# Last norm, router and ranks as one flow, a ring of eight expert weights, and expert rows stored from ScalarE's queue

## What is computed

```
h2 = rms_norm(xl, norm2_gain) * (1.0 + sc2) + sh2          # 512 tokens x 1024
g_logits = h2 @ w_rg + b_rg                                 # 4 groups
e_logits = h2 @ w_re + b_re                                 # 4 groups x 8 experts
g_sel = argmax(g_logits); g_w = softmax(g_logits)[g_sel]
top_w, top_i = top_k(softmax(e_logits[g_sel]), 2)           # two experts of the chosen group
top_w = top_w / sum(top_w) * g_w
y = sum over the two experts e: top_w[e] * ((silu(h2 @ w_gate[e]) * (h2 @ w_up[e])) @ w_down[e])
xl = xl + g2 * y
```

## Time and profile before

| | us |
|---|---|
| median of 3 runs | 2468.18 (2465.8 to 2471.98) |
| profiled execution, its own time | 2464.07 |
| its span, first to last instruction | 2462.2 |
| TensorE matmul busy | 2201.4 (89% of the span) |
| VectorE busy | 900.0 (37%) |
| ScalarE busy | 509.3 (21%) |
| GpSimd busy | 121.4 (5%) |

### The profile page before, as it was taken

One profiled execution on the slowest core, in us unless ns is written; L12 is line 12 of the kernel. 1 busy time (PEld: TensorE's weight loads), 2 busy tenths in 40 slices (PEclk: granted clock), 3 DMA queues, 4 the chain that ended last, 5 costly groups with the idle time before them and its releaser, 6 DMA issues. The chain is left out here.

```text
span 2462.2 us, 35642 instructions
## 1 busy us (share of the span) xinstructions
PE 2201.4 (89%) x15256; PEld 1344.8 (55%) x15256; DVE 900.0 (37%) x1867; ACT 509.3 (21%) x1036; POOL 121.4 (5%) x152
## 2 busy tenths in 40 slices
PE   7999999888998998999999787896976699999995
PEld 3445575445775343585865454783874454444442
DVE  3661064324333013068335556537544411111102
ACT  1000161131122012242112545224211010000001
POOL 0000000004210000000000000300400000000001
PEclk9999999999999999999999998888976799999997
DMA  3222201100003851111130000000004599999995
GB/s 131 77 77 77 77 2 43 61 30 27 28 28 111 343 187 43 43 52 35 44 125 26 1 1 27 3 14 14 4 18 179 210 405 427 426 427 426 428 426 234
DMA packets 48205, 328.45 MB, mean 133 GB/s; under 512 B 5552, under 2 KB 10288, under 8 KB 33840
## 3 DMA queue, kind: packets, MB, share of 16 engines
q1 hardware_dynamic: 46896, 321.96, 33.5%
q0 software_dynamic: 1152, 4.19, 0.5%
HBM read 311.45 MB, written 14.68 MB: 132 GB/s over the span
## 5 line engine op out<-in xcount | busy, mean ns | idle before, releaser
L3188 PE MATMUL psum<-m_ring,m_xg 128*64 128x512 f32 x1024 | 230.3, 604 | 19.9 <-issue 18.7
L258 PE MATMUL psum<-h,wring 128*128 128x512 f32 (+1 forms) x448 | 172.8, 535 | 16.8 <-PEq L93 12.4
L481 PE MATMUL psum<-h,wring 128*128 128x512 f32 x384 | 167.7, 600 | 7.2 <-PEq L93 7.2
L3188 PEld LDWEIGHTS psum<-m_ring,m_xg 128*64 128x64 f32 x1024 | 79.5, 139 | 167.6 <-issue 166.3
L3173 PE MATMUL psum<-m_sel,m_htok 128*128 128x128 f32 x1024 | 122.8, 279 | 17.8 <-DVE m_sel L3164 17.8
L3173 PEld LDWEIGHTS psum<-m_sel,m_htok 128*128 128x128 f32 x1024 | 118.5, 194 | 30.4 <-DVE m_sel L3164 18.2
L258 PEld LDWEIGHTS psum<-h,wring 128*128 128x128 f32 x448 | 84.3, 194 | 84.0 <-issue 73.5
L481 PEld LDWEIGHTS psum<-h,wring 128*128 128x128 f32 x384 | 73.9, 193 | 101.0 <-issue 101.0
L3214 PE MATMUL psum<-m_ring,m_hid_t 128*64 128x512 f32 x512 | 115.0, 602 | 0.9 <-ACT m_hid_t L3312 0.9
L3198 DVE TENSOR_TENSOR m_hid<-m_sg,psum 64x512 f32<-64x512 f32 x32 | 22.1, 691 | 227.4 <-ACT m_sg L3194 227.4
L2293 PE MATMUL psum<-h,wring 128*128 128x256 f32 (+1 forms) x288 | 96.5, 486 | 1.3 <-PEq L93 1.2
(11 more groups left out here) (566 smaller groups left out, 3597.9 us busy)
## 6 DMA issues: line engine op xcount, KB each, us to landing
m_ring<-in_w_gate SPq DMA_DIRECT2D x32, 2048.0 KB, 23.4
m_ring<-in_w_up SPq DMA_DIRECT2D x32, 2048.0 KB, 22.4
m_ring<-in_w_down SPq DMA_DIRECT2D x32, 2048.0 KB, 20.4
wring<-in_w1f SPq DMA_DIRECT2D x60, 512.0 KB, 3.6
ada_ring<-in_w_ada SPq DMA_DIRECT2D x12, 2048.0 KB, 10.3
wring<-in_w2f SPq DMA_DIRECT2D x31, 512.0 KB, 3.5
expert_rows<-m_rows SPq DMA_DIRECT2D x16, 512.0 KB, 22.9
wring<-in_w1v SPq DMA_DIRECT2D x12, 512.0 KB, 3.5
```

The source lines that it names most:

```text
L258: m = nc.tensor.matmul(place(t, out), lhs, rhs, start=(k == 0), stop=(k == KD - 1))
L481: m = nc.tensor.matmul(K.psum[:, banks[t % 4]], ws.weights(first + t, k), h[:, k], start=(k == 0), stop=(k == KD - 1))
L3188: m = nc.tensor.matmul(K.psum[i * SLOTS:(i + 1) * SLOTS, UP + s], W.xg[:, k, s], w[:, k], start=(k == 0), stop=(k == KD - 1))
```

## The change

`last_norm` takes in the logits and the transposes. Tile by tile: VectorE scales into one of four slots, ScalarE adds the shift, TensorE multiplies the tile as moving operand by the router's matrix (one matmul of 36 rows x 512 columns) and turns its four blocks, and VectorE copies the turned tile while it scales the next. The logits come out with experts on partitions; ScalarE adds the bias, four small transposes turn them back, and VectorE copies them (`lg`). The router follows in the same stage and no second stage is opened. It picks the group's logits with two instructions in place of seven and hands over the sum of both choices. The ranks come from four matmuls (up to 128 columns), the totals from four more. `rank` is now one higher, and the slots that it is compared with too (`count1`).

The rest of `place` (positions, further lots) becomes a generator whose five pieces VectorE runs in the experts' stage, one in each of the first five pairs, between its selection and the copy of the rows. Clearing the spare rows moves to the stage `po2`. The ring has eight slots. The row store is issued by ScalarE, after it has copied the next pair's gathered tokens. The buffers `sg` and `rows` now lie in `rstd` and `tmp`, and `hm` has four tiles in place of eight, which frees the space for the slot.

```diff
-def last_norm(nc, K, x, out, gain, shift, bank, loads, weights):
+def last_norm(nc, K, x, hm, h_tok, gain, shift, wr, br, lg_t, lg, count1, loads, weights):
+    SUMS, LOGITS, BACK, NB = 7, 0, 1, 4
+    slot = lambda k: hm[:, k % NB]
+    bank = lambda k: 2 + k % NB
...
     def scalar(eng, sem):
         yield 0.0
-        roots(nc, eng, sem, K, bank, S, 0, 0)
+        roots(nc, eng, sem, K, SUMS, S, 0, 0)
         for k in range(KD):
             eng.wait_ge(sem["scaled"], k + 1)
-            nc.scalar.activation(out(k), out(k), ACT.Identity, bias=shift[:, k:k + 1])
+            nc.scalar.activation(slot(k), slot(k), ACT.Identity, bias=shift[:, k:k + 1]).then_inc(sem["normed"], 1)
+        eng.wait_ge(sem["loaded"], 16 * len(loads))
+        eng.wait_ge(sem["summed"], 1)
+        nc.scalar.activation(lg_t, K.psum[:n_lg, LOGITS], ACT.Identity, bias=br).then_inc(sem["biased"], 1)
+
+    def tensor(eng, sem):
+        yield 0.0
+        eng.wait_ge(sem["loaded"], 16 * len(loads))
+        for k in range(KD):
+            eng.wait_ge(sem["normed"], k + 1)
+            m = nc.tensor.matmul(K.psum[:n_lg, LOGITS], wr[:, k], slot(k), start=(k == 0), stop=(k == KD - 1))
...
+            for t in range(TT):
+                m = nc.tensor.transpose(K.psum[:, bank(k), t * P:(t + 1) * P], slot(k)[:, t * P:(t + 1) * P], K.ident)
+            m.then_inc(sem["turned"], 1)
+        eng.wait_ge(sem["biased"], 1)
+        for t in range(TT):
+            m = nc.tensor.transpose(K.psum[:, BACK, t * n_lg:(t + 1) * n_lg], lg_t[:, t * P:(t + 1) * P], K.ident[:n_lg, :n_lg])
+        m.then_inc(sem["back"], 1)
...
-    return Program(["loaded", "rooted", "scaled"], sync=sync, scalar=scalar, vector=vector)
+        for k in range(NB):
+            scale(k)
+        for k in range(KD - 1):
+            copy(k)
+            if k + NB < KD:
+                scale(k + NB)
+        eng.wait_ge(sem["back"], 1)
+        nc.vector.tensor_copy(lg[:].rearrange("p t n -> p (t n)"), K.psum[:, BACK, :TT * n_lg]).then_inc(sem["logits"], 1)
+        copy(KD - 1)
```

In the router (new functions `picks` and `chosen` name the choices and spread them over the 32 experts):

```diff
-        link(nc.vector.tensor_tensor(es, el[:, :, 0:8], over_heads(fg[:, :, 0], 8), ALU.mult))
-        for g in range(1, N_GRP):
-            link(nc.vector.tensor_tensor(t8, el[:, :, 8 * g:8 * g + 8], over_heads(fg[:, :, g], 8), ALU.mult))
-            link(nc.vector.tensor_tensor(es, es, t8, ALU.add))
+        link(nc.vector.tensor_tensor(of_groups(el), of_groups(el), over_heads(fg, 8), ALU.mult))
+        link(nc.vector.tensor_reduce(es, el.rearrange("p t (g e) -> p t e g", g=N_GRP), AX.X, ALU.add))
...
+        link(nc.vector.tensor_tensor(f12, f1, f2, ALU.add))
+        chosen(nc, both, f12, fg).then_inc(sem["both"], 1)
...
+        nc.vector.tensor_tensor(rank, K.psum[:, bank, 0:N_EXP * TT].rearrange("p (e t) -> p e t", t=TT), both, ALU.mult)
...
+        nc.vector.tensor_copy(cnt, K.psum[:, totals, 0:N_EXP])
```

In the experts' part:

```diff
-    N = 7
+    N = 8
...
         def _(sync):
-            def store(i):
-                sync.wait_ge(sem["rcopied"], i + 1)
-                sync.dma_start(result[i * P:(i + 1) * P, :], W.rows[:]).then_inc(sem["stored"], 16)
             for c in range(weights.N, per * pairs):
                 sync.wait_ge(used, c - weights.N + 1)
                 weights.request(sync, c)
-                if c >= per + weights.N - 1 and (c - weights.N + 1) % per == 0:
-                    store((c - weights.N + 1) // per - 1)
-            for i in range((per * pairs - weights.N) // per, pairs):
-                store(i)
...
+            def store(i):
+                act.wait_ge(sem["rcopied"], i + 1)
+                act.dma_start(result[i * P:(i + 1) * P, :], W.rows[:]).then_inc(sem["stored"], 16)
...
                 if i < pairs - 1:
                     copy(i + 1)
+                store(i)
...
                 if i + 2 < pairs:
                     select(i + 2)
+                next(rest, None)
                 dve.wait_ge(used, per * i + per)
...
-        weave(nc, "po2", last_project(nc, K, a, wide, mix_r, x1, gain, (K.mixed, 2)), end)
+        zeros, result = sb("m_zeros", [P, D], pr), nc.dram_tensor("expert_rows", (LOTS * SLOTS, D), F32).ap()
+        weave(nc, "po2", last_project(nc, K, a, wide, mix_r, x1, gain, (K.mixed, 2)), end, clear_lots(nc, K, zeros, result))
```

More of the change, by code:

```diff
@@ L452, in vector, with scale @@
     def vector(eng, sem):
         yield 0.0
-        eng.wait_ge(sem["rooted"], 2)
-        for k in range(KD):
-            nc.vector.scalar_tensor_tensor(out(k), x[:, k], gain[:, k:k + 1], K.rstd[:, 0], ALU.mult, ALU.mult).then_inc(sem["scaled"], 1)
-    return Program(["loaded", "rooted", "scaled"], sync=sync, scalar=scalar, vector=vector)
+        def scale(k):
+            if k >= NB:
+                eng.wait_ge(sem["turned"], k - NB + 1)
+            nc.vector.scalar_tensor_tensor(slot(k), x[:, k], gain[:, k:k + 1], K.rstd[:, 0], ALU.mult, ALU.mult).then_inc(sem["scaled"], 1)
@@ new lines, in copy @@
+        def copy(k):
+            eng.wait_ge(sem["turned"], k + 1)
+            nc.vector.tensor_copy(h_tok[:, :, k * P:(k + 1) * P], K.psum[:, bank(k)].rearrange("p (t n) -> p t n", t=TT)).then_inc(sem["copied"], 1)
+        nc.vector.tensor_scalar(count1, K.count, 1.0, None, ALU.add)
+        eng.wait_ge(sem["rooted"], 2)
+        for k in range(NB):
[5 more added lines that the diff above has]
+        eng.wait_ge(sem["back"], 1)
@@ L2881, in sync, with picks, router, tensor @@
             eng.dma_start(result[N_EXP * SLOTS + x * P:N_EXP * SLOTS + x * P + P, :], zeros[:]).then_inc(sem["cleared"], 16)
+        yield 1.0
         eng.wait_ge(sem["cleared"], 16 * n)
     return Program(["zero", "cleared"], gpsimd=gpsimd, sync=sync)
-def router(nc, K, lg, first, second, weights, scr):
+def picks(scr):
+    return scr[:, :, 8:12], scr[:, :, 32:40], scr[:, :, 40:48]
+def router(nc, K, lg, both, rank, weights, cnt, scr, bank, totals):
     gl, el = lg[:, :, 0:N_GRP], lg[:, :, N_GRP:]
-    gx, ind, fg = scr[:, :, 0:4], scr[:, :, 4:8], scr[:, :, 8:12]
-    es, e2, f1, f2, t8 = (scr[:, :, 16 + 8 * i:24 + 8 * i] for i in range(5))
+    gx, ind = scr[:, :, 0:4], scr[:, :, 4:8]
+    fg, f1, f2 = picks(scr)
+    es, e2, f12 = (scr[:, :, 16 + 8 * i:24 + 8 * i] for i in (0, 1, 4))
     one = [scr[:, :, 56 + i] for i in range(8)]
     gmax, gsum, mx, m1, m2, ratio, w1, w2 = one
+    of_groups = lambda x: x.rearrange("p t (g e) -> p t g e", g=N_GRP)
+    def tensor(eng, sem):
+        yield 0.7
+        ranks = K.psum[:, bank, 0:N_EXP * TT].rearrange("p (e t) -> p e t", t=TT)
+        eng.wait_ge(sem["both"], 1)
+        nc.tensor.matmul(K.psum[:, bank, 0:N_EXP * TT], K.upto, both.rearrange("p e t -> p (e t)"), start=True, stop=False)
+        for u in range(TT - 1):
+            m = nc.tensor.matmul(ranks[:, :, u + 1:], K.ones, over_heads(both[:, :, u], TT - 1 - u), start=False, stop=(u == TT - 2))
+        m.then_inc(sem["ranked"], 1)
+        for u in range(TT):
+            m = nc.tensor.matmul(K.psum[:, totals, 0:N_EXP], K.ones, both[:, :, u], start=(u == 0), stop=(u == TT - 1))
+        m.then_inc(sem["ranked"], 1)
     def vector(eng, sem):
@@ L3024, in experts @@
+def experts(nc, K, a, x1, mod, gains, out, result):
+    RANKS = 7
     ph = ExitStack()
```

193 lines of the change are left out of this document (84 added, 109 removed).

## The result

The changed kernel takes 2430.35 us (median of 4 runs, 2426.9 to 2433.76) where the kernel before takes 2468.65 beside it (4 runs, 2465.8 to 2471.98): ratio 0.9844, 95% interval 0.9824 to 0.9865. A second set on another occasion gave 2427.47 (5 runs) and 0.9856 (0.9837 to 0.9876). The profiled execution takes 2428.45 us (span 2426.6), 35.6 less than the one of before. Forecast were 2434.0 and 34.2 less.

A forecast was written before the change was run, and what follows sets the result against it. Transfers at 427 GB/s behind the experts' stage's first request were taken to set the end. 30.5 + 4.9 - 1.2 = 34.2 us off the 2468.2 us median gives 2434.0 us, range 2429 to 2439.

The forecast's parts named there:

- The bound: Experts' stage: the end is its first request, plus all bytes behind it at 427 GB/s, plus a way to the end.
- Part 1: Norm to ranks: first gather at 1908.9 instead of 1939.42, 30.5 us earlier, the first request moving as much.
- rival A: Norm: TensorE's clock stays low, tiles end 7.6 us later, saving 26.6, time 2441.6 us; chance 0.25.
- part 4: Placing pieces in the experts' stage and zeros moved to `po2` are hidden: nothing, at worst 1 us.
- Part 2: Eighth ring slot fills in idle time; 88 tiles instead of 89 behind the first request, 4.9 us less.
- Part 3: Row store from ScalarE: nothing in the steady state, 1.2 us more at the end, or 0.
- the sign of taking turns: Experts' stage: a store lands in under 5 us if the DMA queues take turns.
- Rival C: Experts' stage: ScalarE held by its DMA issue, silu late, slower than before; 2497 us at 12 us an issue; chance 0.02.
- The sum: Whole kernel: 30.5 + 4.9 - 1.2 = 34.2 us saved, last rows copy at 2395.8, median 2434.0 us.
- Rival B: Experts' stage: two queues share worse than one; at 420 GB/s 7.5 us more, 2441.5 us; chance 0.20.
- D: Norm's flow is longer by unseen hand-overs between engines: 1 us a tile, 8 us, 2442 us; chance 0.20.

The follow-up runs named there:

- The doubled stores: Changed kernel with each pair's results stored a second time from ScalarE's queue into another tensor; median 2447.7 us.
- the ring of seven: Changed kernel with seven weight-tile slots in place of eight (`N = 7`), nothing else; median 2435.8 us.

## Why the prediction was right

**The bound** was read rightly. In the ten profiles with eight slots and one store a pair the first request lies anywhere from 1920 to 1951, and the last weight tile lands 458.2 to 458.9 us behind it, the last rows copy comes after 466.1 to 467.4. The bytes alone, 192.4 MB at 427 GB/s, are 450.6; the other 8 are the same in all. The doubled stores were paid at 18.0 us of 18.4.

**Part 1, 30.5 us forecast, 30.24 measured at the request.** That it comes so close is in part luck: counted from the end of the projection's last product, 1879.89 before, the request is 29.1 us earlier in the first profile and 31.4 in the second (there that product ends at 1880.37). The spread is the clock's, which fell in the norm of the one and not of the other, and rose sooner in the gather of the second. Two sizes in the forecast were off and cancelled. I had the clock low from the start and up after 5.4 us at 1888.5; it was still up for the first tile, fell, and rose near 1887. A tile takes 1.57 us at the full clock, not 1.32, since the sum of durations left out what goes by where products and transposes change places. The choice took 5.0 us, as forecast. The gather began 0.8 us earlier than forecast, which is less than the 1.16 that the whole stage was early, and then lasted 10.33 us where the one before took 9.21, because the clock rose later in it. Before, on TensorE's timeline:

```profile
1939.42 9.21 PE L3173 MATMUL psum<-m_sel,m_htok 128*128 128x128 f32 x64 [17.85 <-DVE m_sel L3164]
```

The rule behind rival A, that of the Trainium skill (TensorE: Matmul & The Clock Gate, "Part 4: PE-mode transpose"), did not hold the clock down in this mix: with transposes for a third of the stream it rose from 0.50 to 1.00 near 1887.

**What the forecast left unsaid** is that this part depends on part 4. I priced the zeros' move at nothing, for what it costs in the projection, and that is right: from the issue of its first load to the end of its last product the stage takes 46.7 to 46.9 us in the four profiles without the zeros in it and 45.4 to 47.0 in the ten with them. But left in the norm's stage they would have kept the gather back to 1933.5, and most of the 30 us with it. Half a line on which engine ends the stage would have shown it: in the earlier trace rows SP is at the zeros for 23.10 us, under a chain that was longer then.

**Part 2, 4.9 us forecast.** 5.0 to 5.1 by the ring of seven, at the landing of the last weight tile. The idle time ahead of the request was 6.5 us, forecast under 6.

**Part 3, 1.2 us of loss forecast, none measured**: less than 0.5 us in *q to w*, with either sign, in three pairs of kernels that differ in the queue alone. The store landed after 10.3 us, between the under 5 that I had set as the sign of taking turns and the 22.9 of standing in line; in the steady state the answer was right, nobody waits. Rival C is out, by ScalarE's timeline:

```profile
2006.68 0.34 ACTq L3317 DMA_DIRECT2D expert_rows<-tmp  x1
2012.23 0.59 ACT L3221 ACTIVATE rstd<-psum 64x512 f32<-64x512 f32 x1 [12.87 <-PE psum L3215]
```

The issue takes 0.34 us, and 5.2 us later the silu is still waiting for TensorE; its idle time of 12.87 us is the one that it had before. Of part 4, the pieces of the chain fit: VectorE still waits 2.0 to 3.7 us ahead of its rows copy in the five pairs that have one, and 6.3 in the next.

**The sum** was 34.2, the profiles differ by 35.6. Without the 1.2 the forecast would have been 35.4. The medians differ by 38.3, and by 36.4 in the second set; of this I explain no more than the profiles show. Counted from the end of the projection's last product the last rows copy is 34.75 us earlier in the first profile and 38.08 in the second. The 3.3 us between the two are the clock's doing, in the norm, the gather and the last product. *q to e* shrank by 5.7 and 6.6 us, of which 5.5 and 5.4 are *q to w*: the slot, and 0.4 that no run explains. The rest is the last down product, 8.66 us before, 8.74 and 7.09 after. It takes the longer time where the clock falls to 0.50 for some 3 us in it. Why it falls in some profiles and not in others, after pauses of 1.4 and 0.9 to 1.5 us, wasn't tried. Rival B did not happen (427 GB/s throughout), A for two tiles at most, and of D only the quarter of a us a tile.

## What to carry to other kernels

Where transfers set the pace, look for the stretch in which they stand still and ask what ends it; a chain brought forward, or a buffer added, is worth just what it takes off that stretch. By the same account more of it gives nothing once nothing is left there, but no run went beyond that point. A stage ends with its slowest engine, the one that only issues or waits for DMAs included: before moving work into or out of a stage, write down when each engine, SP too, would be done. A store that nobody waits for may stand in any queue, as long as it lands before its buffer is written again.

## What the hardware showed that I had not expected

- Eight stores asked for right behind eight tiles kept SP's queue for 34.01 us, 4.3 each; behind seven tiles, and begun 4.1 us after the last of them, 23.10; in the projection, with idle DMA engines, 8.24.
- A store on ScalarE's queue beside a full SP queue lands after 10.3 us, a second one behind it after 16.4; on SP's own queue after 26.1 (medians). The rate of all stays at 427 GB/s. The Trainium skill's taking of turns (DMA: Bandwidth & Descriptors, "Queues, rings and completion order") agrees in that the store passes tiles that were asked for earlier.
- With the same extra matmuls beside the choice, and the same pauses of 1.0 and 1.4 us around them, the clock fell within the gather where the norm had begun at the lower clock, and did not fall where extra matmuls had kept it up since before the norm. What decides it stays open.
- The clock can fall behind short pauses: in the last down product it goes to 0.50 for some 3 us in five of the thirteen profiles with single stores, both of the kernel before among them. In these five TensorE had run at 1.00 for some 37 us, with no pause above 1.5 us. The product takes 1.5 to 1.7 us longer for it.
